# First stage of a one-core transformer kernel: weight rows of 2 KB, paired q heads, one product for each compressed k/v, gate columns beside the rotary key's

## The reference

```python
h = rms_norm(x, ev_mix_norm[i]) @ ev_w_in[i]          # 1024 x 1720
(q, k_c, v_c, k_s, v_s, k_w, v_w, gates, c_q, c_kv, k_rope) = jnp.split(h, split_at, axis=-1)
# widths: 512, then six times 128, then 24, 256, 128, 32
o_nsa = nsa_mixer(q, k_c, v_c, k_s, v_s, k_w, v_w, gates, ...)
o_mla = mla_mixer(c_q, c_kv, k_rope, ...)
x = x + jnp.concatenate([o_nsa, o_mla], axis=-1) @ ev_w_out[i]
x = x + swiglu(rms_norm(x, ev_ffn_norm[i]), ffn_w_gate[i], ffn_w_up[i], ffn_w_down[i])
```

## Time and profile before

| | |
|---|---|
| median of 3 runs | 2886.78 us |
| lowest and highest | 2883.68, 2887.09 us |
| span of the profiled execution, first to last instruction | 2878.1 us |
| mean granted TensorE clock | 0.986 |
| TensorE matmul busy | 2783.3 us (97%) |
| VectorE, ScalarE, POOL busy | 1044.2 (36%), 710.7 (25%), 1520.0 us (53%) |
| DMA over the span | 372.16 MB, 129 GB/s |

### The profile page before, as it was taken

The page is one execution under the profiler, slowest core; times in us unless marked ns, Lnnn a source line. Parts: engine busy times, 40 slices in busy tenths (PEclk is TensorE's granted clock), DMA queues, the critical chain, the costliest instruction groups (busy, mean ns, idle before and its releaser), DMA issues.

```text
span 2878.1 us, 38168 instructions
## 1 busy us (share of the span) xinstructions
PE 2783.3 (97%) x14585; PEld 2315.1 (80%) x14585; DVE 1044.2 (36%) x2085; ACT 710.7 (25%) x1771; POOL 1520.0 (53%) x1648
## 2 busy tenths in 40 slices
PE   7899999999999989999999989899999998999999
PEld 3545888888878889999999977678888786788887
DVE  1036653312235520000000144737357237465372
ACT  2135762100120111111111033532112225421120
POOL 2121026767777641231282136368879663588786
PEclk9999999999999989999999999999999999999999
DMA  8460003333353259989989931243332322433321
GB/s 189 105 175 15 16 22 96 92 91 103 95 161 103 74 156 281 248 256 266 262 242 267 294 106 45 99 137 94 101 101 81 93 61 94 111 100 95 103 92 48
DMA packets 543428, 372.16 MB, mean 129 GB/s; under 512 B 32510, under 2 KB 496199, under 8 KB 542346
## 3 DMA queue, kind: packets, MB, share of 16 engines
q1 hardware_dynamic: 525216, 322.63, 39.9%
q0 software_dynamic: 11440, 33.00, 3.7%
q10 hardware_dynamic: 6586, 14.03, 2.0%
HBM read 336.60 MB, written 32.41 MB: 128 GB/s over the span
## 4 chain that ended last, share of the span: by engine, by line
PE 91%; DVE 3%; DMA 2%; ACT 2%; issue 1%; ACTq 0%; DVEq 0%; POOL 0%; SPq 0%; POOLq 0%
PE bank L600 18%; PE bank L602 18%; PE bank L601 18%; PE bank L760 15%; PE bank L1194 7%; PE bank L854 2%; PE bank L832 2%; DMA ring<-in_ev_w_in 1%; PE bank L802 1%; PE bank L842 1%; PE bank L816 1%; DMA ring<-in_moe_w_up 1%; ACT x_hi L1601 1%; PE bank L959 1%; PE bank L1024 1%
## 5 line engine op out<-in xcount | busy, mean ns | idle before, releaser
L2048 POOL TENSOR_TENSOR unit_parts<-ring,unit_parts 128x512 fp32r<-128x512 f32 x580 | 805.5, 1389 | 48.4
L2046 POOL TENSOR_SCALAR unit_parts<-ring 128x512 fp32r<-128x512 f32 x580 | 424.8, 732 | 495.7 <-PE bank L602 324.9
L600 PE MATMUL bank<-x_hi,unit_parts 128*128 128x512 f32 x1408 | 555.3, 394 | 19.3 <-DVE x L2565 10.3
L602 PE MATMUL bank<-x_hi,unit_parts 128*128 128x512 f32 x1408 | 550.4, 391 | 0.0
L601 PE MATMUL bank<-x_lo,unit_parts 128*128 128x512 f32 x1408 | 550.4, 391 | 0.0
L760 PE MATMUL bank<-arena,ring 128*128 128x160 f32 x2816 | 385.4, 299 | 2.7 <-DMA ring<-in_moe_w_up 1.9
L760 PEld LDWEIGHTS bank<-arena,ring 128*128 128x128 f32 x2816 | 383.0, 190 | 3.3 <-DMA ring<-in_moe_w_up 2.1
L600 PEld LDWEIGHTS bank<-x_hi,unit_parts 128*128 128x128 f32 x1408 | 265.9, 189 | 77.8 <-DVE x L2565 11.5
L600 PE MATMUL bank<-unit_parts,hid_parts 128*128 128x512 f32 x784 | 308.1, 393 | 3.3 <-DVE hid_parts L2587 2.6
L602 PEld LDWEIGHTS bank<-x_hi,unit_parts 128*128 128x128 f32 x1408 | 265.7, 189 | 55.9
L601 PEld LDWEIGHTS bank<-x_lo,unit_parts 128*128 128x128 f32 x1408 | 265.8, 189 | 55.1 <-issue 1.0
(11 more groups left out here) (360 smaller groups left out, 3337.1 us busy)
## 6 DMA issues: line engine op xcount, KB each, us to landing
ring<-in_moe_w_gate SPq DMA_DIRECT2D x88, 512.0 KB, 5.4
ring<-in_moe_w_up SPq DMA_DIRECT2D x88, 512.0 KB, 6.9
ring<-in_moe_w_down SPq DMA_DIRECT2D x64, 704.0 KB, 5.0
ring<-in_w_up SPq DMA_DIRECT2D x88, 512.0 KB, 5.2
ring<-in_w_down SPq DMA_DIRECT2D x16, 1024.0 KB, 5.1
ring<-in_od_w_in SPq DMA_DIRECT2D x24, 512.0 KB, 4.9
ring<-in_ffn_w_gate SPq DMA_DIRECT2D x22, 512.0 KB, 4.0
ring<-in_ffn_w_up SPq DMA_DIRECT2D x22, 512.0 KB, 5.3
```

Source lines behind the costliest of these rows:

```text
L600: pe.matmul(ps, a[0], b[0], start=start, stop=False)
L602: return pe.matmul(ps, a[1], b[0], start=False, stop=stop)
L2046: pool.tensor_scalar(hi, raw, 1.0, 1.0, ALU.mult, ALU.mult).then_inc(S("units_rounded"), 1)
L2048: pool.tensor_tensor(lo, raw, hi.bitcast(F32), ALU.subtract).then_inc(S("units_split"), 1)
```

## The change

q is fetched as two chunks of 512 rows of W_in, each row 512 columns (2 KB); the columns of k_s, v_s, k_w and v_w likewise (`WideRows`). Group qt then takes columns 128t to 128t + 127, which are heads 2t and 2t + 1 of one group, and POOL loads `q_stack` in four DMAs of every second head. Each compressed k/v gets one product with both heads, and ScalarE copies each head twice from it, at once and shifted. The gate columns stand behind c_kv and the rotary key in one chunk; their product is rows 96 to 119 of the bank of the rotary key, ScalarE makes the sigmoid there, TensorE turns them in four transposes ahead of mq0, and ScalarE copies them out. v_s and v_w are a moving operand of two pieces of 128 columns with 128 between them. The table of constants is issued behind the second chunk, not the first. Before it the stage took 9 chunks to the end of ckv, now 7.

```diff
+            def fmajor_by(key, weights):
+                ps = claim(key)
+                for k in range(KD):
+                    ins = pe.matmul(ps[:, :], weights(k), xnT[:, k, :], start=k == 0, stop=k == KD - 1)
+                fill(ins, key)
+            class WideRows:
+                def __init__(self, W):
+                    self.W, self.at, self.rows = W, [], []
+                def __call__(self, k):
+                    if k // 4 == len(self.rows):
+                        self.rows.append(chunk((0, 4, 512, self.W[512 * (k // 4):512 * (k // 4) + 512, :])))
+                        self.at.append(len(chunks) - 1)
+                    return self.rows[k // 4][:, k % 4 * 512:k % 4 * 512 + 512]
+                def release(self, key):
+                    for n in self.at:
+                        chunks[n][2] = filled_sem(key)
...
-                if name in ("q0", "q2"):
+                if name[0] == "q":
                     t0 = int(name[1])
-                    parts = [(64 * (2 * (t - t0) + gr), KD, 64, W_in[:, 256 * gr + 64 * t:256 * gr + 64 * t + 64], 256)
-                             for t in (t0, t0 + 1) for gr in range(2)]
-                    mm1.w = chunk(*parts)
-                    fmajor(key, mm1.w, 256, 0, P)
-                elif name in ("q1", "q3"):
-                    fmajor(key, mm1.w, 256, P, P, release=True)
+                    if t0 == 0:
+                        mm1.q = WideRows(W_in[:, 0:512])
+                    fmajor_by(key, lambda k: mm1.q(k)[:, P * t0:P * t0 + P])
+                    if t0 == 3:
+                        mm1.q.release(key)
...
-                    for kv in range(2):
-                        at = 512 + P * kv
-                        w = chunk(*[(64 * r, KD, 64, W_in[:, at + 64 * (r // 2):at + 64 * (r // 2) + 64], 256)
-                                    for r in range(4)])
-                        fmajor(("cz", kv, 0), w, 256, 0, P)
-                        fmajor(("cz", kv, 1), w, 256, P, P, release=True)
-                    mm1.w = chunk((0, KD, P, W_in[:, 768:896], 256), (P, KD, P, W_in[:, 1024:1152], 256))
-                    fmajor(key, mm1.w, 256, 0, P)
+                    w = chunk((0, KD, 256, W_in[:, 512:768]))
+                    fmajor(("cz", 0), w, 256, 0, P)
+                    fmajor(("cz", 1), w, 256, P, P, release=True)
+                    mm1.kv = WideRows(W_in[:, 768:1280])
+                    fmajor_by(key, lambda k: mm1.kv(k)[:, 0:P])
                 elif name == "kw":
...
-                    w = chunk((0, KD, P, W_in[:, 896:1024], 256), (P, KD, P, W_in[:, 1152:1280], 256))
-                    wg = chunk((0, KD, 24, W_in[:, 1280:1304]))
                     for t in range(NT):
                         ps = claim(("vs", t))
                         for k in range(KD):
-                            pe.matmul(ps[:, 0:256], xnT[:, k, t * P:(t + 1) * P], w[:, k * 256:(k + 1) * 256],
-                                      start=k == 0, stop=k == KD - 1)
-                        for k in range(KD):
-                            ins = pe.matmul(ps[:, 256:280], xnT[:, k, t * P:(t + 1) * P], wg[:, k * 24:(k + 1) * 24],
-                                            start=k == 0, stop=k == KD - 1)
+                            both = mm1.kv(k).rearrange("p (b a n) -> p b a n", b=2, a=2)[:, :, 1, :]
+                            ins = pe.matmul(ps[:, 0:256], xnT[:, k, t * P:(t + 1) * P], both, start=k == 0, stop=k == KD - 1)
                         fill(ins, ("vs", t))
...
+                    fmajor_by(key, lambda k: mm1.kv(k)[:, 2 * P:3 * P])
+                    mm1.kv.release(key)
...
-                    w = chunk((0, KD, 160, W_in[:, 1560:1720]))
+                    w = chunk((0, KD, 160, W_in[:, 1560:1720], 184), (160, KD, 24, W_in[:, 1280:1304], 184))
                     ps = claim(("kr",))
-                    fill(fmajor(None, w, 160, P, 32, rows_at=64, reuse=ps), ("kr",))
-                    fmajor(key, w, 160, 0, P, release=True)
+                    fill(fmajor(None, w, 184, P, 56, rows_at=64, reuse=ps), ("kr",))
+                    fmajor(key, w, 184, 0, P, release=True)
...
+                        ps = claim(("gates",))
+                        wait_drained(pe, ("kr",))
+                        for t in range(NT):
+                            ins = pe.transpose(ps[:, t * 24:(t + 1) * 24], krT[96:120, t * P:(t + 1) * P],
+                                               c("ident")[96:120, 96:120])
+                        fill(ins, ("gates",))
...
-            pe.wait_ge(S("q_stack_in"), 32)
+            pe.wait_ge(S("q_stack_in"), 64)
...
-                if n == 0:
+                if n == 1:
                     sp.dma_start(cst[:, EARLY:], A["constants"][:, EARLY:]).then_inc(S("tables_in"), 16)
...
-                        if g["name"] in ("cq", "kc"):
+                        if g["name"] == "kc":
                             ln_exp_table()
...
+                        ps = wait_filled(act, ("cz", kv))
                         for gr in range(2):
-                            key = ("cz", kv, gr)
-                            ps = wait_filled(act, key)
-                            z = Z[:, 2 * kv + gr, :]
-                            act.activation(z[0:64, :], ps[0:64, :], ACT.Copy)
-                            drain(act.activation(z[64:128, 0:T - 1], ps[64:128, 1:T], ACT.Copy), key)
+                            z, of = Z[:, 2 * kv + gr, :], ps[64 * gr:64 * gr + 64, :]
+                            act.activation(z[0:64, :], of, ACT.Copy)
+                            ins = act.activation(z[64:P, 0:T - 1], of[:, 1:T], ACT.Copy)
+                        drain(ins, ("cz", kv))
...
-                        act.activation(vsw[:, t, :], ps[:, 0:256], ACT.Copy)
-                        drain(act.activation(gat[:, t * 24:(t + 1) * 24], ps[:, 256:280], ACT.Sigmoid), ("vs", t))
+                        drain(act.activation(vsw[:, t, :], ps[:, 0:256], ACT.Copy), ("vs", t))
...
+                    drain(act.activation(krT[96:120, :], ps[96:120, :], ACT.Sigmoid), ("kr",))
...
             for half in range(2):
-                pool.dma_start(q_stack[64 * half:64 * half + 64].rearrange("p (g h) t -> p g h t", g=2),
-                               heads_dram[half, :, 0:4 * T].rearrange("(g p) (h t) -> p g h t", g=2, h=4))\
-                    .then_inc(S("q_stack_in"), 16)
+                for g in range(2):
+                    pool.dma_start(q_stack[64 * half:64 * half + 64, g:HN:2, :],
+                                   heads_dram[half, 64 * g:64 * g + 64, 0:4 * T].rearrange("p (h t) -> p h t", h=4))\
+                        .then_inc(S("q_stack_in"), 16)
```

More of the change, by code:

```diff
@@ L940, in mm1 @@
                 elif name == "ks":
-                    for kv in range(2):
-                        at = 512 + P * kv
-                        w = chunk(*[(64 * r, KD, 64, W_in[:, at + 64 * (r // 2):at + 64 * (r // 2) + 64], 256)
-                                    for r in range(4)])
-                        fmajor(("cz", kv, 0), w, 256, 0, P)
-                        fmajor(("cz", kv, 1), w, 256, P, P, release=True)
-                    mm1.w = chunk((0, KD, P, W_in[:, 768:896], 256), (P, KD, P, W_in[:, 1024:1152], 256))
-                    fmajor(key, mm1.w, 256, 0, P)
+                    w = chunk((0, KD, 256, W_in[:, 512:768]))
[3 more added lines that the diff above has]
+                    fmajor_by(key, lambda k: mm1.kv(k)[:, 0:P])
                 elif name == "kw":
-                    ks_w = mm1.w
-                    ks_chunk = len(chunks) - 1
-                    w = chunk((0, KD, P, W_in[:, 896:1024], 256), (P, KD, P, W_in[:, 1152:1280], 256))
-                    wg = chunk((0, KD, 24, W_in[:, 1280:1304]))
                     for t in range(NT):
@@ L958, in mm1 @@
                         for k in range(KD):
-                            pe.matmul(ps[:, 0:256], xnT[:, k, t * P:(t + 1) * P], w[:, k * 256:(k + 1) * 256],
-                                      start=k == 0, stop=k == KD - 1)
-                        for k in range(KD):
-                            ins = pe.matmul(ps[:, 256:280], xnT[:, k, t * P:(t + 1) * P], wg[:, k * 24:(k + 1) * 24],
-                                            start=k == 0, stop=k == KD - 1)
+                            both = mm1.kv(k).rearrange("p (b a n) -> p b a n", b=2, a=2)[:, :, 1, :]
+                            ins = pe.matmul(ps[:, 0:256], xnT[:, k, t * P:(t + 1) * P], both, start=k == 0, stop=k == KD - 1)
                         fill(ins, ("vs", t))
-                    release_by(("vs", NT - 1))
-                    release_by(("vs", NT - 1), 2)
-                    fmajor(key, ks_w, 256, P, P)
-                    chunks[ks_chunk][2] = filled_sem(key)
+                    fmajor_by(key, lambda k: mm1.kv(k)[:, 2 * P:3 * P])
+                    mm1.kv.release(key)
                 elif name == "cq":
@@ L1706, in pre1 @@
                         ps = wait_filled(act, ("vs", t))
```

(12 more changed lines are left out.)

## The result

| | before | after |
|---|---|---|
| median (range, runs) | 2885.48 us (2883.68 to 2887.09, 4) | 2869.13 us (2867.22 to 2870.97, 4) |
| span of the profiled execution | 2878.1 us | 2866.2 us |
| mean granted clock | 0.986 | 0.985 |
| TensorE matmul busy | 2783.3 us | 2761.9 us |

The ratio is 0.9943, 95% interval 0.993 to 0.9956: 16.4 us faster. 2873.0 was forecast, 2866 to 2881; the case of the sum came true. Between the two profiles its terms are off by more than its total: the first stage gained 3.8 us more than the sum has, a stall of 6.0 was in no term, and the total is off by 1.9.

What follows compares the result with a forecast made beforehand. TensorE, with 91% of the chain, was taken to bound the kernel. The terms -13.76 - 6.80 + 0.2 - 8.41 + 13.2 + 1.8 = -13.8 us, applied to the 2886.78 median, gave 2873.0, range 2866 to 2881.

Steps and rivals of the forecast that it cites:

- the case of the sum: Whole kernel: all terms add to -13.8 us, giving 2873.0, own range 2869 to 2879; chance 72%.
- Compressed k/v, -13.76: First stage: two of four fmajor calls go, each sixteen matmul records of 6.88 us; -13.76 us.
- gates -6.80: First stage: four groups of 16 gate records, 1.70 us each, go by joining another product; -6.80 us.
- transposes +0.2: First stage: four new 24-column gate transposes, about half covered by TensorE idling; +0.2 us, bounds 0 and 1.0.
- The wait before L959, -8.41: Before the value products: 6.63 us idling for the gate fetch and 1.78 of slow clock go; -8.41 us.
- Landing near 30 us: First stage: x, five chunks and tables, 9.5 MB, land near 30 us, before the table write starts.
- rival 3: A kv chunk misses the table write's start; TensorE stands 20.3 us plus 1.8 of slow clock, 2895; chance 7%.
- cq, "101.2; I take 97 to 101": First stage: cq's fetch lands at 97 to 101, TensorE wants it at 101.2; nothing, up to 5 us high.
- The ring, +13.2 and +1.8: Late layer 0: two chunks fewer put a weight chunk in a held slot, delaying 32 moves +13.2; slow clock +1.8.
- Rival 1: Late layer 0: the move wait does not bite; -13.8 - 15.0, 2858; chance 8%.
- Rival 2: First stage: cq waits for its weights behind the table write; +2 to +8 us, 2875 to 2881; chance 8%.
- Rival 4: Value products: the split moving operand costs double; +14.2 us, 2887, no change; chance 5%.

Runs made afterwards that it cites:

- a_kv_late: a_moves with the ring advanced one slot before the k/v rows, so their second chunk is issued during the table write; 2879.28 us, ratio 0.9978.
- a_split_values: a_moves with two of the four value products put behind kw, in front of cq; 2854.07 us, ratio 0.989.
- b_both: Kernel before with one product per compressed k/v and gate columns behind the rotary key; old short rows and late-layer slots kept; 2860.26 us, ratio 0.9907.
- a_reset: Changed kernel with the ring set back to slot 0 where each late layer's narrow phase begins; 2857.79 us, ratio 0.9905.
- a_moves: Changed kernel with late layer 0's 32 moves issued one chunk earlier, ahead of the chunk meeting the held slot; 2856.57 us, ratio 0.99.
- b_one_cz: Kernel before with one product for each compressed k/v instead of two; gate fetch and chunk numbers kept; 2892.05 us, ratio 1.0019.

## Why the prediction was right, and where it was not

**What ScalarE's stall says of my base.** I took 8.7 us as what lies around the span. In every later run the time is the span plus 1.8 us. The other 6.9 were that this execution was faster than the median one. So the trace was not of the typical run, and the comparison of the two profiles (-11.9) understates the change by what the stall cost. Against the second profile of before it would be -21.5, which overstates it, as that execution was 3.6 us above its median. The medians give -16.4, and the sum of the two places that the change does touch is -32.64 + 15.48 = -17.2.

**Compressed k/v, -13.76, gates -6.80, transposes +0.2.** TensorE's own work is as counted, and the transposes cost nothing: the matched distance is -31.49 ahead of them and -31.65 behind, as the 0.45 us of idling there is gone. But the terms were added as if each were worth itself. The runs say: +6.0, -11.1, and -24.8 for both. The sum was right because both parts are in the change; as a price list it would mislead.

**The wait before L959, -8.41.** Right in size here. It is two waits, the gates' fetch (4.2 us of it) and a bank (2.45), and the second went only because one product for each compressed k/v takes two banks out of the turn. I hadn't seen that: for these 2.45 us the term came right by luck. With the gates' part alone 4.2 went, and none of the slow clock behind the wait.

**Landing near 30 us, rows of 2 KB.** Right, about 29. The 256-byte rows landed at 37.7: rival 3 lay 1.8 us away for them and 10 us away for the change, and costs 22.7 us where I gave 22.1. The fetch made late in a_kv_late landed near 91, not 97.

**cq, "101.2; I take 97 to 101".** Landed at 98; a_split_values shows it as a bound at 98.69. The slow clock at cq, which I left in place, did not come in the changed kernel (13.97 for 15.67) and came in a_kv_late and b_both with the same wait of 2.44. That 1.7 us, 0.4 at the start, some 0.35 in the pace of the value products and 1.7 at the clock at the stage's end, less 0.5 lost in the heads ahead of it, make up most of the -32.64 against -28.8. The two of 1.7 are a matter of where the clock falls.

**The ring, +13.2 and +1.8.** The mechanism was right to the slot. The wait came to 13.96 - 1.55 = 12.4: I had all 32 moves at 21.15 us and they took 20.23, the pace of the lower bound. The clock was undersized: 6.74 - 3.67 = 3.1 for 1.8. I had priced it by the 6.63 us gap; behind one of 14 us the whole of glu ran at 1.2 GHz. Together 15.5 for 15.0.

**Rivals.** Rival 1 is what a_reset and a_moves build (forecast 2858, measured 2857.8 and 2856.6). Rival 2 did not come: cq's weights landed at 98, and cq waited for its bank until 100.22. Rival 4 is ruled out by 13.98 us for 64 records. On the rule of the Trainium skill (DMA: Bandwidth & Descriptors, Queues, rings and completion order) that a queue keeps its turn for a packet of typically 9 to 17 descriptors: this case's traces disagree. From 74 to 90 us of the kernel before q10 and q1 start 304 and 303 packets, and their running counts never part by more than three; the 2 KB rows of a_kv_late go about one for one as well. The "ten times faster" that I drew from the rule doesn't follow from it either: with turns of equal length on both queues the fetch advances as with one for one, and it gains only where the write's turns are the shorter ones.

**Open.** What ends ScalarE's "remote" waits isn't shown; no run was made to move them. The price of a single stall can't be read cleanly either, since the clock differs around it.

## What to carry to other kernels

When a fixed-order ring feeds the engines, count its slots modulo its size far behind the edit: two chunks fewer in the first 100 us cost 15 us at 1850, and one term in the place where the moves are issued gave them back. Two edits in front of one late transfer aren't additive: one alone can be worth less than nothing, so take away the late transfer together with the work. Moving its rival, the table write, only moved the wait, and cost 23 us. And take a second profile of the kernel before if the span and the median stand further apart than in the runs that follow.

## What the runs showed of the hardware

- The write of 2.5 MB in packets of 2560 bytes took 55 us in the kernel before and 58 in the changed one, on eight of the 16 DMA engines. A fetch issued during it has one half at once and the other one packet for one of the write's: 96 KB in rows of 96 bytes took 42.6 us, 1 MB in rows of 1 KB 44.0 (cq in b_both), 1 MB in rows of 2 KB some 36 (a_kv_late). A fetch costs TensorE nothing if it lands before the write, or if it isn't wanted until the write's end, as cq's in the changed kernel.
- Fewer matmuls made the kernel slower (b_one_cz, +6.0 us): the idle time that took their place also cost clock behind it (1.25 us in the first sixteen records).
- The granted clock after short idle times isn't a fixed function of their length: with 2.44 us before cq it fell in b_both (granted 0.50 from 100.9 to 104.0, cq 15.60 us) and in a_kv_late (15.67 us), and not in the changed kernel (1.00 from 100.2 to 104.0, 13.97 us).
